# A third chunk lent to the seventh expert, the mask added out of PSUM, and probabilities divided on ScalarE before plain transposes

## The chip, the core and the metric

The kernel runs on one core of one Trainium2 chip. The metric is device time in microseconds (us) of one execution. Everything is float32; products of the front are made from two-part (high and low) float32r numbers to keep precision, those of the experts in plain float32.

## The reference, cut to what matters

One layer of an encoder over 256 tokens of width 1024: a combined projection, three attentions side by side, a gated merge, and a top-4-of-32 expert layer.

```python
h = rms_norm(x, attn_norm_g[l]); proj = h @ w_in[l]        # q, k, v of three branches, three gates
# A: 8 heads of 64 on a (4 x 64) token grid, window of 16 columns, bias by offset
# B: 12 heads of 64 in three groups (dilation 1, 4, 16), T5 bias, one softmax over the three groups
# C: 4 heads of 128 over 256 memory tokens
p = softmax(s + bias)            # per head; 256 x 256 scores; out = p @ v
merged = sum(gate_b * (branch_b @ w_branch_b)); x = x + merged @ w_out[l]
# experts: h = rms_norm(x); top 4 of 32 by router
gu = xb @ w_gu[e] + b_gu[e]      # 1024 -> 2048, 8 MB of weights per expert
g = min(gu[:, :1024], 7); u = clip(gu[:, 1024:], -7, 7)
a = (u + 1) * (g * sigmoid(1.702 * g)); y = a @ w_dn[e] + b_dn[e]     # 4 MB per expert
x = x + y_weighted; return rms_norm(x, final_norm_g)
```

## The kernel before, in words

All engine programs are written out by hand, each engine in its own order, with semaphores between them. Two parts follow each other.

**The front.** A list `FRONT` of 42 weight chunks of 1 MB (memory, input projection, branch and output weights) goes through a ring of 6 slots. SyncE (SP) issues all loads in one queue, chunk i when chunk i-6 is used (`chunk_used`). For each chunk ScalarE makes the high part (`high_part`, L1060, two halves), GpSimd the low part by subtraction (L568, two halves), and TensorE makes three products high-high, low-high, high-low; the last needs the low part (`parts_of_chunk`, L690). `high_part(i+2)` stands in ScalarE's iteration i, since the parts have two buffers. "Wide" pairs of chunks fill whole rows of 512.

The attention is a pipeline laid between chunks: `STEP_AFTER` says after which chunk i step s comes. There are 12 units of two heads: two C, four A, six B (groups 1 and 2 of B, `own_parity`, have half the keys: 128 columns in place of 256). Step s does on TensorE, in this order, `head_scores(s)` (L598), `turn_probs(s-3)` (L620) and `attend(s-4)` (L641). On VectorE (from L1345) it adds the relative image and, for A, the column mask `na_mask` (L1371), takes the row maximum (L1373) and its negative (`neg_max`, L1381), copies half of the turned probabilities (L1388), and at the steps of `SCALE_AT` inverts the sums of an output (L1397) and multiplies the identity by them (L1401). On ScalarE `exps(u)` (L1080) stands at the end of the step's iteration once all units of an output have their scores, and copies of the other half (L1159) and of the output (L1169) beside it. `turn_probs` turns the unnormalised exponentials by a matmul against a diagonal matrix of inverse sums, so that division and transpose are one operation; it waits for `scale_ready`.

**The experts.** 32 experts, 12 chunks of 1 MB each (8 gate/up, 4 down), in one order made by `transfers()` (L158), stream through a ring of 20 slots; chunk c is loaded when chunk c-20 and those beside it in one transfer are used. TensorE does gate/up of expert n and then down of n-1. Between the front and the experts the tokens are normalised (GpSimd and ScalarE, L573, L1188), routed and gathered. SP's order there: `FIRST_LAP` (chunks 2, 12, 14, 18, 16), a wait for the normalised tokens (`normed`, `tile_normed`, `sums_open`), the lent chunks, chunk 20, the stream.

Two chunks of the sixth expert, `LENT`, don't go through the ring. They are loaded early to memory that is idle by then (the tokens `x`, the bias staging, small tables), and `weights_landed` (L923) waits for them by semaphores of their own. After them, `x` takes the down bias and the final gain, which `DOWN_BIAS_AT` adds in four of the experts.

## Time and profile before

| | us |
|---|---|
| median of 3 runs | 1232.18 (1231.66 to 1232.54) |
| profiled execution, its own time | 1229.89 |
| span of that execution in the trace | 1228.1 |
| TensorE busy | 1174.6 (96%), 6225 instructions |
| VectorE busy | 267.5 (22%) |
| ScalarE busy | 253.0 (21%) |
| GpSimd busy | 207.2 (17%) |
| HBM read | 453.13 MB, 370 GB/s over the span |

Busy shares are averages over two stages with different limits; GpSimd's work, for one, lies wholly in the first quarter. An instruction's duration in a row contains its latency, so that for instructions in a row the distance between starts is less than the mean duration. The granted clock of TensorE is 0.987 of full speed in the mean. In the page's second part the span is cut into 40 slices of 30.7 us; the digits there are tenths.

### The profile page before, as it was taken

Reading aid. Unit: us, or ns where it says so; the run is one execution under the profiler, and the core shown is the slowest. Engines: PE = TensorE matmul, PEld = TensorE weight load, DVE = VectorE, ACT = ScalarE, POOL = GpSimd, SP = SyncE. Lnnn points to the kernel's source line nnn. Section 1 sums busy time; section 2 is a strip of 40 time slices with the busy share of each in tenths; the row PEclk is TensorE's granted clock in tenths of the full one; section 3 lists DMA queues with packets and bytes.
Section 4 is the critical chain, followed back from the end, with each engine's and each line's share of the span. In section 5 each row is a group of like instructions: output and inputs, shape, how many; then the busy total and the mean of one; then the engine's idle time right before and its main releaser. Section 6 shows DMA issues by size and latency. Waiting matters only on the chain.

```text
span 1228.1 us, 14301 instructions
## 1 busy us (share of the span) xinstructions
PE 1174.6 (96%) x6225; PEld 605.9 (49%) x6225; DVE 267.5 (22%) x543; ACT 253.0 (21%) x531; POOL 207.2 (17%) x89
## 2 busy tenths in 40 slices
PE   8999999999999999999999999999998998999996
PEld 8989887899433433333333333333333333333332
DVE  3148252232411112111111121111111111111112
ACT  6446455344301011100101010000100000000101
POOL 5865766686100000000000000000000000000000
PEclk9999999999999999999999999999999999999999
DMA  9753544599999999999999999999999999999995
GB/s 316 241 168 122 167 155 137 185 357 389 347 428 430 425 430 415 430 430 429 432 432 431 428 430 431 430 429 430 433 429 431 427 432 428 430 429 427 430 427 231
DMA packets 61703, 455.14 MB, mean 371 GB/s; under 512 B 5081, under 2 KB 33657, under 8 KB 43464
## 3 DMA queue, kind: packets, MB, share of 16 engines
q1 hardware_dynamic: 61640, 454.22, 90.0%
q8 instruction: 50, 0.82, 0.3%
q14 instruction: 13, 0.11, 0.0%
HBM read 453.13 MB, written 1.07 MB: 370 GB/s over the span
## 4 chain that ended last, share of the span: by engine, by line
PE 63%; DMA 33%; DVE 1%; POOL 1%; ACT 1%; issue 0%; DVEq 0%; SPq 0%; ACTq 0%; POOLq 0%
PE ps L579 62%; DMA arena<-in_expert_w_gate_up 29%; DMA arena<-in_expert_w_down 3%; POOL w_parts L568 1%; PE ps L895 1%; PE ps L889 0%; DVE arena L1371 0%; DMA arena<-in_mem 0%; DVE x_normed L1542 0%; PE ps L702 0%; PE ps L586 0%; ACT arena L1087 0%; PE ps L679 0%; DVE arena L1401 0%; DVE arena L1267 0%
## 5 line engine op out<-in xcount | busy, mean ns | idle before, releaser
L579 PE MATMUL ps<-arena,gathered_T 128*64 128x512 f32 x2034 | 471.2, 611 | 36.3 <-DMA arena<-in_expert_w_gate_up 36.3
L579 PE MATMUL ps<-arena 128*64 128x512 f32 (+8 forms) x1650 | 335.7, 534 | 4.1 <-DVE arena L1401 1.6
L579 PEld LDWEIGHTS ps<-arena,gathered_T 128*64 128x64 f32 x2034 | 144.9, 140 | 302.0 <-issue 273.3
L579 PEld LDWEIGHTS ps<-arena 128*64 128x64 f32 (+3 forms) x1650 | 132.2, 153 | 198.9 <-issue 191.6
L568 POOL TENSOR_TENSOR w_parts<-arena,w_parts 128x1024 fp32r<-128x1024 f32 x42 | 102.9, 2474 | 46.8 <-ACT w_parts L1067 37.7
L568 POOL TENSOR_TENSOR w_parts_odd<-arena,w_parts_odd 128x1024 fp32r<-128x1024 f32 x38 | 90.8, 2409 | 45.7 <-ACT w_parts_odd L1067 45.7
L1486 DVE TENSOR_SCALAR arena<-arena 128x128 f32<-128x128 f32 x64 | 19.3, 344 | 315.3 <-PE ps L889 315.3
L1209 ACT COPY arena<-ps 128x256 f32<-128x256 f32 x32 | 11.9, 372 | 358.8 <-PE ps L889 358.8
L1492 DVE TENSOR_SCALAR arena<-ps 128x512 f32<-128x512 f32 x32 | 22.1, 692 | 273.1 <-PE ps L579 273.1
L579 PEld LDWEIGHTS ps<-arena,x_normed 128*128 128x128 f32 x512 | 59.5, 192 | 24.8 <-issue 24.3
L1200 ACT ACTIVATE gathered_T<-ps,g_cols 128x128 f32<-128x128 f32 x128 | 36.5, 368 | 170.1 <-PE ps L579 170.1
L579 PE MATMUL ps<-arena,x_normed 128*128 128x128 f32 x512 | 65.4, 281 | 0.2 <-DVE arena L1443 0.2
L579 PE MATMUL ps<-w_parts_odd,h_T_parts 128*128 128x256 f32 (+1 forms) x360 | 59.1, 322 | 0.0
L1501 DVE COPY arena<-ps 128x512 f32<-128x512 f32 x32 | 22.1, 691 | 155.1 <-PE ps L895 155.1
L579 PEld LDWEIGHTS ps<-w_parts_odd,h_T_parts 128*128 128x128 f32 x360 | 51.5, 188 | 7.1 <-issue 1.8
L1217 ACT COPY arena<-ps 128x512 f32<-128x512 f32 x31 | 18.2, 586 | 172.3 <-PE ps L579 172.3
L1067 ACT CAST w_parts<-arena 128x1024 fp32r<-128x1024 f32 x40 | 39.9, 1047 | 49.2 <-PE ps L579 49.0
L1067 ACT CAST w_parts_odd<-arena 128x1024 fp32r<-128x1024 f32 x38 | 37.9, 1047 | 40.8 <-PE ps L579 40.3
L1213 ACT ACTIVATE arena<-arena 128x512 f32<-128x512 f32 x32 | 20.3, 633 | 109.6 <-DVE arena L1492 109.6
L579 PE MATMUL ps<-w_parts,h_T_parts 128*128 128x512 f32 (+1 forms) x216 | 41.1, 347 | 0.0
L579 PEld LDWEIGHTS ps<-w_parts,h_T_parts 128*128 128x128 f32 x216 | 33.7, 188 | 6.2 <-issue 0.6
L579 PE MATMUL ps<-h_T_parts,w_parts 128*128 128x256 f32 x288 | 35.5, 282 | 0.0
(181 smaller groups left out, 727.1 us busy)
## 6 DMA issues: line engine op xcount, KB each, us to landing
arena<-in_expert_w_gate_up SPq DMA_DIRECT2D x53, 4096.0 KB, 39.4
arena<-in_expert_w_down SPq DMA_DIRECT2D x62, 2048.0 KB, 38.8
arena<-in_expert_w_gate_up SPq DMA_DIRECT2D x21, 2048.0 KB, 12.4
arena<-in_w_in SPq DMA_DIRECT2D x29, 1024.0 KB, 5.4
arena<-in_w_out SPq DMA_DIRECT2D x4, 1024.0 KB, 11.3
arena<-in_expert_w_down SPq DMA_DIRECT2D x4, 1024.0 KB, 41.0
arena<-in_w_mem_kv SPq DMA_DIRECT2D x3, 1024.0 KB, 12.3
arena<-in_w_branch_a SPq DMA_DIRECT2D x2, 1024.0 KB, 5.1
```

Source lines behind the costliest of these rows:

```text
L568: last = nc.gpsimd.tensor_tensor(parts_at(i)[:, 1, half], ring[:, i % FRONT_RING, half], parts_at(i)[:, 0, half].bitcast(F32), ALU.subtract)
L579: return nc.tensor.matmul(out, lhsT, rhs, start=start, stop=stop, **kw)
L895: last = nc.tensor.transpose(ps[:, 2, f * P:(f + 1) * P], sig.rearrange("p (q f) -> p f q", f=4)[:, f, :], ident[:])
L1067: nc.scalar.copy(parts_at(i)[:, 0, half], ring[:, i % FRONT_RING, half]).then_inc(high_ready, 1)
L1200: last = nc.scalar.mul(xt[:, c, 0:width], ps[:, bank, k * P:k * P + width], g_cols[:, 3 * KC + c:3 * KC + c + 1])
L1209: nc.scalar.copy(WT[:, wt_slot, :], ps[:, 3, 0:S]).then_inc(WT_ready, 1)
L1213: nc.scalar.activation(sig, gate_c, ACT.Sigmoid, scale=ALPHA).then_inc(sig_ready, 1)
L1217: nc.scalar.copy(y_sb, ps[:, bank, :]).then_inc(y_ready, 1)
L1486: last = vec.tensor_scalar(PW[:, tt, :].rearrange("p (a s) -> p a s", a=2), bcast(slots, 1, 2), key_tile[:, tt, e], w_sel[:, tt, e], ALU.i ...
L1492: vec.tensor_scalar(gate_c, ps[:, 0, :], LIMIT, None, ALU.min).then_inc(gate_ready, 1)
L1501: vec.tensor_copy(aT, ps[:, 2, :].rearrange("p (f s) -> p f s", f=4)).then_inc(aT_ready, 1)
```

## The change

Three edits, with what they need.

- `LENT` has three chunks (5, 6 and 7 of gate/up) of the seventh expert in place of two of the sixth; `transfers()` splits that expert's second transfer so that each of them stands alone. The third goes to `behind_work`, the last 2048 columns of a working area 240 columns longer, which the merged tokens' parts occupy until the last chunk of the front is used; SP issues it behind `FIRST_LAP`, ahead of the wait for the normalised tokens. The down bias is added from expert 10 on.
- A units: VectorE adds the image in place in PSUM, then the mask with PSUM as source and SBUF as destination; `scores_drained` is raised after the mask.
- `turn_probs` makes plain transposes of probabilities that are already divided. ScalarE's `divide(u)` multiplies the exponentials of a unit by the inverse sums in place, at the head of the iteration of step u+3, ahead of `high_part(i+2)`. VectorE makes only the inverse (`inverse_ready`); `scaled_ident` is gone.
- Memory: row statistics move to the working area, `y_sb` becomes the same memory as `gate_c`, for which `move_down` waits for two more semaphores.

```diff
--- before.py
+++ after.py
@@ -52,7 +52,7 @@
 SCORE_SLOT = 8
 SECOND_SPLIT_SLOT = 10
 FRONT_SLOT = 12
-FRONT_WORK = 22784
+FRONT_WORK = 23024
 LATE_PARTS = (39, 41)
 IMAGES = 3
 EXPERT_CHUNKS = 12
@@ -93,15 +93,15 @@
 T5_STORE_AFTER = 11
 STEP_SLOT = {s: i for i, s in STEP_AFTER.items()}
 
-DOWN_BIAS_AT = {9: (0, 0), 10: (0, 1), 11: (1, 0), 12: (1, 1)}
+DOWN_BIAS_AT = {10: (0, 0), 11: (0, 1), 12: (1, 0), 13: (1, 1)}
 IMAGE_AFTER = {u: 9 if u < 2 + IMAGES else STEP_SLOT[u - IMAGES] + FRONT_RING for u in range(2, NU)}
 
 EARLY_AFTER = {36: 0, 38: 4, 39: 6, 40: 8, 41: 10}
 FIRST_LAP = {2: 38, 12: 38, 14: 40, 18: 41, 16: NF}
 FIRST_LONG = 4
 
-LENT_TO = 5
-LENT = (EXPERT_CHUNKS * LENT_TO + 2, EXPERT_CHUNKS * LENT_TO + 3)
+LENT_TO = 6
+LENT = tuple(EXPERT_CHUNKS * LENT_TO + j for j in (1, 2, 3))
 
 QK_DONE, QKV_DONE = {"C": 6, "A": 10, "B": 18}, {"C": 6, "A": 12, "B": 21}
 
@@ -161,7 +161,7 @@
     end_down = [(KC, 2), (KC + 2, 1), (KC + 3, 1)]
     order = [(0, *t) for t in short]
     for n in range(1, EXPERTS):
-        lent = [(0, 4), (4, 2), (6, 1), (7, 1)]
+        lent = [(0, 4), (4, 1), (5, 1), (6, 1), (7, 1)]
         order += [(n, *t) for t in (lent if n == LENT_TO else long if FIRST_LONG <= n < EXPERTS - 1 else short)]
         order += [(n - 1, *t) for t in (down if n < EXPERTS - 1 else end_down)]
     order += [(EXPERTS - 1, *t) for t in end_down]
@@ -214,10 +214,6 @@
         pick_raw = sb("pick_raw", [P, 2, EXPERTS + 1])
         sumsq = sb("sumsq", [P, 4, T])
         rstd = sb("rstd", [P, 4, T])
-        row_max = sb("row_max", [P, NU, 4])
-        neg_max = sb("neg_max", [P, 8, 4])
-        exp_sum = sb("exp_sum", [P, NU, 4])
-        inv_sum = sb("inv_sum", [P, 8, 4])
         ovf = sb("ovf", [P, MAX_OVERFLOW + 1], I32)
         b_tmp = sb("b_tmp", [P, 2, 4])
 
@@ -247,11 +243,13 @@
         pT = area(FRONT0, 2, 2, 2, S)
         image = area(FRONT0 + 2048, IMAGES, 2, IMG)
         na_mask = area(FRONT0 + 2048 + IMAGES * 2 * IMG, 4, GRID_W // 2)
+        stats_at = FRONT0 + 4096
+        row_max, exp_sum = area(stats_at, NU, 4), area(stats_at + 64, NU, 4)
+        neg_max, inv_sum = area(stats_at + 128, 8, 4), area(stats_at + 192, 8, 4)
         v = area(FRONT0 + 4352, T, 1280)
         mv = area(FRONT0 + 6912, T, MEM_HEADS * MEM_HD)
         qkT = area(FRONT0 + 8192, 24, S)
         mkT = area(FRONT0 + 14336, MEM_HEADS, MEM)
-        scaled_ident = area(FRONT0 + 15360, 2, 4, P)
         gates = area(FRONT0 + 16384, T, D)
         onehot = area(FRONT0 + 4352, REL)[0:T5_BUCKETS + 3, :]
         t5_in = area(FRONT0 + 4864, DIL_HEADS)[0:T5_BUCKETS + 3, :]
@@ -299,7 +297,7 @@
         assert place[0] <= FRONT0 + 18688
         router_parts = area(place[0], S)
         sig = moe(512)
-        y_sb, aT = moe(512), moe(4, P)
+        y_sb, aT = gate_c, moe(4, P)
         wT_sel = moe(S)[0:EXPERTS, :]
         pick = split_at("pick", place[0], 2, 2 * BLK)
         moe(2 * 2 * BLK)
@@ -312,6 +310,8 @@
         okeys = moe(T, EXPERTS)
         extra, ends = moe(EXPERTS), moe(EXPERTS)
         ovf_f = moe(MAX_OVERFLOW)
+        behind_work = area(FRONT0 + FRONT_WORK - CHUNK, CHUNK)
+        assert place[0] <= FRONT0 + FRONT_WORK - CHUNK
         final_g, far_iota, b_dn = x[:, 0, :], x[:, 1, :], x[0:EXPERTS, 1, :]
         final = xn[:]
 
@@ -346,7 +346,7 @@
         probs_exp = sem("probs_exp")
         front_evac, wide_done = sem("front_evac"), sem("wide_done")
         scores_ready, scores_drained = sem("scores_ready"), sem("scores_drained")
-        max_ready, exp_done, scale_ready = sem("max_ready"), sem("exp_done"), sem("scale_ready")
+        max_ready, exp_done, inverse_ready, divided = sem("max_ready"), sem("exp_done"), sem("inverse_ready"), sem("divided")
         probs_turned, pT_dve, pT_act = sem("probs_turned"), sem("pT_dve"), sem("pT_act")
         pv_done, out_high, out_low = sem("pv_done"), sem("out_high"), sem("out_low")
         merged_ready = sem("merged_ready")
@@ -380,7 +380,8 @@
 
         x_flat = x[:].rearrange("p t c -> p (t c)")
         bias_flat = bias_raw[:].rearrange("p b c -> p (b c)")
-        lent_pieces = {LENT[0]: [bias_flat[:, 0:512], bias_flat[:, 512:1024], until_ranked[:], until_routed],
+        lent_pieces = {LENT[2]: [behind_work[:, 512 * i:512 * (i + 1)] for i in range(4)],
+                       LENT[0]: [bias_flat[:, 0:512], bias_flat[:, 512:1024], until_ranked[:], until_routed],
                        LENT[1]: [x_flat[:, 512 * i:512 * (i + 1)] for i in range(4)]}
 
         def piece(c, i):
@@ -510,16 +511,18 @@
 
             sp.wait_ge(merged_ready, 4)
             sp.dma_start(iota, bass.AP(t["iota"].tensor, 0, [[0, P], [1, BLK]])).then_inc(iota_in, 16)
+            def lend(c, first, n, place):
+
+                e, j, _ = TRANSFERS[c]
+                src = w_gu[bass.ds(e, 1), :, j * CHUNK + 512 * first:j * CHUNK + 512 * (first + n)].rearrange("o p c -> (o p) c")
+                sp.dma_start(place, src).then_inc(lent_in[c], 16)
+
             for c, used in FIRST_LAP.items():
                 sp.wait_ge(chunk_used, used)
                 if used == NF:
                     load_bias()
                 load_weights(*TRANSFERS[c], ring_slot(c))
-            def lend(c, first, n, place):
-
-                e, j, _ = TRANSFERS[c]
-                src = w_gu[bass.ds(e, 1), :, j * CHUNK + 512 * first:j * CHUNK + 512 * (first + n)].rearrange("o p c -> (o p) c")
-                sp.dma_start(place, src).then_inc(lent_in[c], 16)
+            lend(LENT[2], 0, 4, behind_work)
 
             sp.wait_ge(normed, 3)
             sp.wait_ge(tile_normed, 1)
@@ -618,8 +621,7 @@
                 last.then_inc(scores_ready, 1)
 
             def turn_probs(u):
-                o = OUTPUT_OF[u]
-                pe.wait_ge(scale_ready, o + 1)
+                pe.wait_ge(divided, u + 1)
                 if u == 0:
                     pe.wait_ge(t5_copied, 1)
                 else:
@@ -628,14 +630,12 @@
                 for hh in range(2):
                     if own_parity(u):
                         for tt in range(T):
-                            last = mm(ps[:, 6 + hh, tt * P:(tt + 1) * P], scores[:, u % 4, hh, tt, 0:P],
-                                      scaled_ident[:, o % 2, 2 * hh + tt, :], True, True)
+                            last = nc.tensor.transpose(ps[:, 6 + hh, tt * P:(tt + 1) * P], scores[:, u % 4, hh, tt, 0:P], ident[:])
                         continue
                     for kt in range(T):
                         for tt in range(T):
-                            last = mm(ps[:, 6 + hh, kt * S + tt * P:kt * S + (tt + 1) * P],
-                                      scores[:, u % 4, hh, tt, kt * P:(kt + 1) * P], scaled_ident[:, o % 2, 2 * hh + tt, :],
-                                      True, True)
+                            last = nc.tensor.transpose(ps[:, 6 + hh, kt * S + tt * P:kt * S + (tt + 1) * P],
+                                                       scores[:, u % 4, hh, tt, kt * P:(kt + 1) * P], ident[:])
                 last.then_inc(probs_turned, 1)
 
             def attend(u):
@@ -923,7 +923,7 @@
             def weights_landed(c):
 
                 if c in LENT:
-                    pe.wait_ge(lent_in[c], {LENT[0]: 48, LENT[1]: 16}[c])
+                    pe.wait_ge(lent_in[c], {LENT[0]: 48, LENT[1]: 16, LENT[2]: 16}[c])
                 else:
                     pe.wait_ge(landed[ring_slot(c)], 16 * fills_through(c))
 
@@ -1088,6 +1088,15 @@
                                                     accum_out=exp_sum[:, u, 2 * hh + tt:2 * hh + tt + 1])
                 last.then_inc(exp_done, 1)
 
+            def divide(u):
+                o = OUTPUT_OF[u]
+                act.wait_ge(inverse_ready, o + 1)
+                for hh in range(2):
+                    for tt in range(T):
+                        p = scores[:, u % 4, hh, tt, 0:P if own_parity(u) else S]
+                        last = nc.scalar.mul(p, p, inv_sum[:, o, 2 * hh + tt:2 * hh + tt + 1])
+                last.then_inc(divided, 1)
+
             def move_wide(i, tt):
 
                 kind, n = FRONT[i - 1]
@@ -1109,6 +1118,8 @@
                     act.wait_ge(wide_done, WIDE_LAST.index(i) + 1)
                     move_wide(i, 0)
                 merging = ONLY_B < i < OUT0
+                if i in STEP_AFTER and 0 <= STEP_AFTER[i] - TURN_LAG < NU:
+                    divide(STEP_AFTER[i] - TURN_LAG)
                 if i + 2 < NF and not merging:
                     high_part(i + 2)
                 if i - 1 in STEP_AFTER and STEP_AFTER[i - 1] in LAST_OF_B:
@@ -1212,8 +1223,10 @@
                 act.wait_ge(gate_ready, n + 1)
                 nc.scalar.activation(sig, gate_c, ACT.Sigmoid, scale=ALPHA).then_inc(sig_ready, 1)
 
-            def move_down(chunks, bank):
+            def move_down(chunks, bank, n):
                 act.wait_ge(chunk_used, chunks + NF)
+                act.wait_ge(prod_ready, n + 1)
+                act.wait_ge(sig_ready, n + 1)
                 nc.scalar.copy(y_sb, ps[:, bank, :]).then_inc(y_ready, 1)
 
             for n in range(EXPERTS):
@@ -1223,7 +1236,7 @@
                     move_gathered(n % 2, XT[:, (n // 2 + 1) % 2], 2 * BLK, n + 2)
                 sigmoid(n)
                 if n:
-                    move_down(down_chunk(n - 1) + 4, 3)
+                    move_down(down_chunk(n - 1) + 4, 3, n)
             move_weights(EXPERTS - 1, (EXPERTS - 1) % 2)
             n_over = act.value_load(ovf[0:1, MAX_OVERFLOW:MAX_OVERFLOW + 1], min_val=0, max_val=MAX_OVERFLOW)
             with act.If(0 < n_over):
@@ -1233,7 +1246,7 @@
                             move_gathered(half, XT[:, 0], BLK, b * 2 + (EXPERTS + half))
                         move_weights(b + EXPERTS, 1)
                         sigmoid(b + EXPERTS)
-                        move_down(b * EXPERT_CHUNKS + (ALL_CHUNKS + EXPERT_CHUNKS), 3)
+                        move_down(b * EXPERT_CHUNKS + (ALL_CHUNKS + EXPERT_CHUNKS), 3, b + EXPERTS)
 
             nc.scalar.activation(b_tmp[:, 0, 0:1], eps[:], ACT.Sqrt)
             for tt in range(T):
@@ -1352,7 +1365,7 @@
                             dve.wait_ge(image_in[b], 16 * ((s - 2) // IMAGES + 1))
                         for tt in range(T):
                             src = ps[:, 2:4, tt * S:(tt + 1) * S]
-                            dst = scores[:, s % 4, :, tt, :]
+                            dst = src if kind_u == "A" else scores[:, s % 4, :, tt, :]
                             if kind_u == "C":
                                 last = vec.tensor_copy(dst, src)
                             elif own_parity(s):
@@ -1362,13 +1375,16 @@
                                 rel = image[:, b, :, 1 - tt:1 - tt + S].rearrange("p h (j e) -> p h e j", e=2)
                                 by_parity = "p h (e j) -> p h e j"
                                 last = vec.tensor_tensor(dst.rearrange(by_parity, e=2), src.rearrange(by_parity, e=2), rel, ALU.add)
+                        if kind_u == "A":
+                            link(last)
+                            dve.wait_ge(consts_in, 96)
+                            by_column = "p (t e r c) -> p (t e) r c"
+                            for hh in range(2):
+                                biased = ps[:, 2 + hh, :].rearrange(by_column, t=T, e=2, c=GRID_W // 2)
+                                masked = scores[:, s % 4, hh].rearrange("p t k -> p (t k)").rearrange(by_column, t=T, e=2, c=GRID_W // 2)
+                                last = vec.tensor_tensor(masked, biased, bcast(na_mask[:], 2, 4), ALU.add)
                         last.then_inc(scores_drained, 1)
                         dve.wait_ge(scores_drained, s + 1)
-                        if kind_u == "A":
-                            dve.wait_ge(consts_in, 96)
-                            for hh in range(2):
-                                masked = scores[:, s % 4, hh].rearrange("p t (e r c) -> p (t e) r c", e=2, c=GRID_W // 2)
-                                link(vec.tensor_tensor(masked, masked, bcast(na_mask[:], 2, 4), ALU.add))
                         width = P if own_parity(s) else S
                         link(vec.tensor_reduce(row_max[:, s, :], scores[:, s % 4].rearrange("p h t k -> p (h t) k")[:, :, 0:width],
                                                AX_X, ALU.max))
@@ -1394,12 +1410,7 @@
                         if UNITS[w][0] == "B":
                             total = b_tmp[:, 1, :]
                             link(vec.tensor_reduce(total, exp_sum[:, w - 2:w + 1, :].rearrange("p u c -> p c u"), AX_X, ALU.add))
-                        link(vec.reciprocal(inv_sum[:, o, :], total))
-                        if o >= 2:
-                            dve.wait_ge(probs_turned, last_unit_of(o - 2) + 1)
-                        for c in range(4):
-                            last = vec.tensor_scalar(scaled_ident[:, o % 2, c, :], ident[:], inv_sum[:, o, c:c + 1], None, ALU.mult)
-                        last.then_inc(scale_ready, 1)
+                        vec.reciprocal(inv_sum[:, o, :], total).then_inc(inverse_ready, 1)
                     u = s - PV_LAG
                     if 0 <= u < NU and u == last_unit_of(OUTPUT_OF[u]):
                         dve.wait_ge(out_high, OUTPUT_OF[u] + 1)
```

## Rows read from the trace of the kernel before

**Rows 1.** The page: the chain's shares, and GB/s in 40 slices of the span.
```profile
PE 63%; DMA 33%; DVE 1%; POOL 1%; ACT 1%; issue 0%; DVEq 0%; SPq 0%; ACTq 0%; POOLq 0%
...
GB/s 316 241 168 122 167 155 137 185 357 389 347 428 430 425 430 415 430 430 429 432 432 431 428 430 431 430 429 430 433 429 431 427 432 428 430 429 427 430 427 231
```

**Rows 2.** The chain in order of time: start, length, what.
```profile
649.30 37.10 DMA arena<-in_expert_w_gate_up
```

**Rows 3.** Windows: length, then each engine's busy time, PEclk, DMA share, GB/s.
```profile
305.00:310.00 5.00, 4.66 (x30) 2.50 (x30) 2.63 (x12) 4.36 (x9) 2.39 (x1) 1.00 0.83 217
310.00:315.00 5.00, 4.82 (x27) 3.08 (x26) 4.12 (x23) 2.48 (x4) 1.46 (x1) 1.00 0.92 368
315.00:320.00 5.00, 5.00 (x36) 3.46 (x37) 4.52 (x15) 2.28 (x8) 0.00 (x0) 1.00 0.89 344
320.00:325.00 5.00, 5.00 (x25) 1.61 (x22) 1.96 (x11) 0.00 (x0) 0.00 (x0) 1.00 0.55 192
```

**Rows 4.** Timeline of the SP queue between front and experts: start, length, issue.
```profile
307.27 0.58 SPq L440 DMA_DIRECT2D arena<-in_expert_w_down  x1
313.76 0.33 SPq L522 DMA_DIRECT2D x_tokens<-in_expert_w_gate_up  x1
...
321.51 0.33 SPq L440 DMA_DIRECT2D arena<-in_expert_w_gate_up  x1
```

**Rows 5.** DMA issues, KB, us to landing; from 391 to 398, then 417 to 425.
```profile
arena<-in_expert_w_down SPq DMA_DIRECT2D x2, 2048.0 KB, 17.5
...
arena<-in_expert_w_down SPq DMA_DIRECT2D x2, 2048.0 KB, 15.7
```

**Rows 6.** Products of probabilities and merge transposes: groups to 330 us, timeline, chain.
```profile
L579 PE MATMUL ps<-arena 128*128 128x128 f32 x160 | 20.7, 281 | 1.7 <-DVE arena L1401 1.6
...
L702 PE MATMUL ps<-ident,x_normed 128*128 128x128 f32 x16 | 2.4, 272 | 0.0
...
91.28 2.05 PE L579 MATMUL ps<-arena 128*128 128x128 f32 x16 [1.63 <-DVE arena L1401]
...
267.65 0.44 PE ps L702 x4
```

**Rows 7.** VectorE groups to 330 us: busy, mean ns, then idle before them.
```profile
L1371 DVE TENSOR_TENSOR arena<-arena 128x512 f32<-128x512 f32 x8 | 15.3, 1913 | 0.3
L1373 DVE TENSOR_REDUCE row_max<-arena 128x4 f32<-128x1024 f32 x8 | 9.8, 1220 | 0.3
...
L1364 DVE TENSOR_TENSOR arena<-ps,arena 128x512 f32<-128x512 f32 x12 | 7.7, 682 | 36.0 <-PE ps L579 36.0
...
L1381 DVE TENSOR_SCALAR neg_max<-row_max 128x4 f32<-128x4 f32 x6 | 5.7, 942 | 0.2
```

**Rows 8.** ScalarE groups to 330 us, scalings by a column vector.
```profile
L1056 ACT ACTIVATE h_T_parts<-ps,g_cols 128x256 fp32r<-128x256 f32 x8 | 3.0, 489 | 0.0
...
L1200 ACT ACTIVATE gathered_T<-ps,g_cols 128x128 f32<-128x128 f32 x8 | 2.3, 368 | 4.3 <-PE ps L579 4.3
```

**Rows 9.** Timeline of all engines around step 3.
```profile
82.84 1.29 DVE L1364 TENSOR_TENSOR arena<-ps,arena 128x512 f32<-128x512 f32 x2 [13.24 <-PE ps L579]
83.01 5.22 POOL L568 TENSOR_TENSOR w_parts<-arena,w_parts 128x1024 fp32r<-128x1024 f32 x2 [0.74 <-ACT w_parts L1067]
...
88.52 1.13 PE L579 MATMUL ps<-arena 64*128 64x256 f32 x8
...
90.27 0.51 ACT L1087 ACTIVATE arena<-arena,neg_max 128x256 f32<-128x256 f32 x1 [6.45 <-DVE neg_max L1381]
...
92.25 0.56 ACT L1098 COPY arena<-ps 128x512 f32<-128x512 f32 x1
```

**Rows 10.** Timeline of TensorE at step 5, of ScalarE and TensorE at step 9.
```profile
109.36 4.84 PE L579 MATMUL ps<-arena 64*128 64x256 f32 x32
...
175.00 1.28 ACT L1102 ACT_TABLE_LOAD   x1
...
176.87 4.31 PE L579 MATMUL ps<-arena 64*128 64x256 f32 x32
```

## The prediction

> **What bounds the kernel now.** I read the page's chain first: 63% of it is TensorE and 33% DMA, and the GB/s line says where each rules: below 200 in slices 3 to 8, then about 430 from the twelfth slice to the last but one [rows 1]. In order of time the chain first stands on an expert weight transfer at 649.30 [rows 2]; before that it is nearly all TensorE. So there are two regimes: the front (attention, to about 305 us) goes at TensorE's pace, the experts in the end at the DMA's.
>
> What matters is from when the DMA is saturated. In windows of 5 us it moves 217, 368, 344 and 192 GB/s between 305 and 325 [rows 3]. The SP queue says why: it issues a chunk at 307.27, the next thing at 313.76 (it waits for the normalised tokens), and chunk 20, which opens the endless stream, at 321.51, when TensorE has used the first two expert chunks [rows 4]. After that the DMA is always behind its slots. The end is therefore (issue of chunk 20) + (bytes after it) / rate + tail, and two things move it: the front's length, one for one, and bytes taken out of the stream.
>
> **The third lent chunk.** The ring holds 20 chunks; a lent chunk is loaded to other memory ahead of the stream and later left out of it. Leaving one out is worth 1.049 MB / 430 GB/s = 2.44 us. Does its load find idle DMA? It is issued behind chunk 16, at 307.9. From 310 to 325 the DMA gives away 5 x (62 + 86 + 238) / 430 = 4.5 us against 430 GB/s [rows 3], so 2.44 fits, and ahead of chunk 20 too: the 1.8 MB issued between 313.76 and 316 need 4.3 us. Does the omission find a backlog? The down transfers of one expert land 17.5 us after their issue, those of the next, with two chunks left out between, 15.7 [rows 5]: the backlog grows by 15.7 + 4.9 - 17.5 = 3.1 per expert. Now three are left out one expert later and none before: 17.5 + 3.1 + 3.1 - 7.3 = 16.4, so the queue doesn't run dry there. Worth -2.4 us; bounds 0 (if it pushes chunk 20 back by its whole length) and -2.5. The expert after which the down bias and the final gain are fetched only shifts their 0.64 MB. That the down result shares memory with `gate_c` adds waits on products that end while the 32 down matmul instructions before that copy still run: 0.
>
> **Plain transposes.** `turn_probs` makes 8 products of 128x128 for eight of the units and 4 for the four others: 80, which are 160 instructions in the group of this shape [rows 6]; 16 of them took 2.05 us at 91.28, 0.128 each. A transpose is one instruction: 4 take 0.44 us in the merge, 0.11 each [rows 6]. What goes is thus every second instruction, 80 x 0.11 = -8.8 us of TensorE time, all in the part of the front in which TensorE is the chain. Bounds: -10.2 (by 0.128), and 0 if a transpose of such an operand holds the array for two slots after all.
> The Trainium skill (TensorE: Matmul & The Clock Gate, Part 4: PE-mode transpose) speaks against it: about 275 ns for a transpose in a kernel, and transposes don't count as busy time for the clock. Laid end to end at that price the 80 would cost 22 us, more than the products. The trace agrees with the figure as the duration of one transpose and not as the price of each in a row, and the window 305 to 310, with transposes in it, has a granted clock of 1.00 [rows 3, 6].
>
> **Mask out of PSUM.** In each of the four A units VectorE adds the image (out of PSUM, 0.68 a time), then the mask, SBUF to SBUF: 1.91 us on average, 2.8 times as long for the same size [rows 7]. It stands beside GpSimd's subtractions, and the one with a PSUM source doesn't suffer. Out of PSUM I take 0.69, bounds 0.65 and 1.91; 8 x 1.2 = -9.8 us of VectorE time. The image addition now writes PSUM, which no row shows: I take 0.68, bounds 0.6 and 1.9. The scalings of the identity go from VectorE, a reciprocal stays. `neg_max` stays too, and 0.94 on average for 128x4 [rows 7] says that it also waits for GpSimd, so of what the mask gives a part is given back: `neg_max` ends when GpSimd's pair ends. That is off TensorE's path except where the walk below says.
>
> **Divides on ScalarE.** The nearest rows are scalings of 128x256, 8 in 3.0 us, and of 128x128, 8 in 2.3 [rows 8]: 1.6 us for a full unit (three at 0.375, the last to its end 0.49), 1.25 for a small one, 8 x 1.6 + 4 x 1.25 = 17.8 us more ScalarE work. Bounds for a full one 1.2 and 2.1. `divide` is queued behind the exps of the step before (which wait for `neg_max`) and ahead of `high_part(i+2)`. TensorE waits for it in `turn_probs`; behind that stand `attend` and the next chunk. Step by step:
> - Step 3. The scores of unit 2 are there at 82.84. Image 1.3, mask 1.4, maximum 1.2: 86.8; `neg_max` then waits for GpSimd, whose pair begins at 83.01 and takes 4.8 undisturbed (5.22 now): 87.9. Exps and the gap to the evacuation 2.0 (90.27 to 92.25), evacuation 0.6, divide 1.6: 92.2. TensorE has the scores of unit 3 out at 88.52 + 1.13 = 89.65 and waited until 91.28 before [rows 6, 7, 9]. Loses 0.9 more.
> - Step 4. Exps after the first GpSimd subtraction of chunk 13, 96.0 to 98.1, divide to 99.7; TensorE is free at 100.1: 0.
> - Step 5. GpSimd's pair for chunk 14 runs to 105.5, so `neg_max` 105.6, exps to 107.7, copy of C 0.5, divide to 109.8; TensorE is free at 109.6 (109.36 + 1.05 now, less 0.8 of lead) [rows 10]. Loses 0.2.
> - Step 9. A table load of 1.28 (at 175.00) and a sigmoid of 0.6 stand ahead of the divide [rows 10]; with the front 4.2 ahead 170.8 + 1.9 + 1.6 = 174.3, and TensorE is there at 173.7. Loses 0.6, and 0.2 of that it loses now. Step 12 has the same pattern with its exps done: 0.2.
> - In the other eight steps the divide is over before TensorE has finished the chunk: 0.
> Sum 0.9 + 0.2 + 0.4 + 0.2 = 1.7, and the front -8.8 + 1.7 = -7.1 (with 2.1 for a divide -5.1; with no wait left -10.4). `high_part` comes up to 1.6 late, but GpSimd has until 2 us into chunk i+2, with chunk i+1 (5.8) and a step's 2 to 4 us before that, and needs 1.0 + 4.8: some 4 to 5 us of slack. Were that cover gone, each divide would be paid in full (rival 2). SP's wait for `scores_drained` ahead of an image load ends 1.4 later in A units, with the next front load due some 4 us after: 0.
>
> Sum: -7.1 - 2.4 = -9.5 us. The profiled execution took 1229.89 around its span of 1228.1; the median of the runs is 1232.18, 0.2% more. The sum is a difference, and I set it against the median: 1222.7.
>
> **Rivals.**
> 1. *The divide becomes the new wait.* In the dense steps of the A and B units it ends 1.0 late in six instead of in one. For it: steps 3 and 5 are on the edge. Against: from 142 us on the exps lie away from the next step. Front -8.8 + 6 = -2.8, in all -5.2: 1227.0.
> 2. *Slower: high parts come late.* If GpSimd's low part of chunk i+2 is what TensorE waits for, each step pays its whole divide: -8.8 + 17.8 - 2.4 = +6.6, 1238.8. It decides from a delay of 4 to 5 us, where I count 1.6.
> 3. *The lent chunk brings nothing*, its load pushing chunk 20 back: -7.1, 1225.1.
> 4. *Transposes don't run closer than the products.* With two slots each the front changes by 0 to +1.7 (longer turns leave the divides more time), with -2.4 in all -1.5: 1230.7, no change. Laid end to end at their own duration, 0.272 [rows 6]: 80 x 0.272 - 17.6 = +4.2, with 1.7 and -2.4 +3.5, 1235.7, slower. Against both: 4 in 0.44.
>
> **Chances.** Forecast 0.67 (its own range 1220 to 1225.5), rival 1 0.12, rival 3 0.08, rival 2 0.04, rival 4 0.06 at no change and 0.03 slower. What this measurement can tell from no change is about 0.2%, 2.5 us: faster 0.87, same 0.06, slower 0.07. The range reaches from -13 (no wait left and both at their better bounds) to the far edge of rival 1: 1219 to 1229.
>
> **What would show it.** The products of the probabilities: 80 instructions in place of 160. Masks at 0.69 in the VectorE group, with PSUM as source. TensorE waits for ScalarE's divide 2.5 us at its first turn, under 1 at two or three others, and not for GpSimd at the steps. Chunk 20 issued 7 us earlier, near 314.4, with 1 MB more moved in the 15 us before it. The forecast is wrong if chunk 20 is issued less than 4 us earlier, or if it is and the end isn't, which would say that the stream's rate or its backlog is not what I take.

## The result, and the profile after

| | before | after |
|---|---|---|
| median of 4 runs, same chip (us) | 1231.92 (1230.72 to 1232.54) | 1218.21 (1216.15 to 1219.22) |
| profiled execution, its own time | 1229.89 | 1218.18 |
| span | 1228.1 | 1216.4 |
| chunk 20 issued | 321.51 | 314.81 |
| last transfer on the chain landed | 1200.75 | 1187.83 |
| very last weights landed | 1215.51 | 1202.47 |

The ratio is 0.9889, 95% interval 0.9875 to 0.9904: 13.7 us faster, where 9.5 were forecast. The direction was right; the time lies 0.8 us below the low end of the range. So something gave 4 us that the sum did not have.

Of the page of after, the chain's shares, to set beside [rows 1]; then the chain in order of time (start, length, what), its first expert transfer and its last transfer:

```profile
PE 66%; DMA 30%; ACT 1%; DVE 1%; issue 1%; POOL 0%; SPq 0%; DVEq 0%; ACTq 0%; POOLq 0%
```

```profile
695.52 38.56 DMA arena<-in_expert_w_gate_up
...
1149.36 38.47 DMA arena<-in_expert_w_down
```

The two regimes are still there, and the end still follows the transfers. "The chain" is the page's chain of work that ended last; behind its last transfer five more land, up to 15 us later, while TensorE still works. The chain comes onto the DMA 46 us later than in [rows 2].

Windows of after, columns as in [rows 3]:

```profile
305.00:310.00 5.00, 4.84 (x37) 3.98 (x37) 4.46 (x18) 1.35 (x4) 0.00 (x0) 1.00 0.97 408
310.00:315.00 5.00, 5.00 (x29) 2.34 (x29) 4.55 (x20) 1.72 (x7) 0.00 (x0) 1.00 0.94 383
315.00:320.00 5.00, 5.00 (x24) 1.65 (x22) 0.36 (x2) 0.00 (x0) 0.00 (x0) 1.00 0.88 324
320.00:325.00 5.00, 5.00 (x32) 2.78 (x30) 0.00 (x0) 0.53 (x3) 0.00 (x0) 1.00 1.01 426
```

The SP queue of after, to set beside [rows 4]; the second line is the third lent chunk, the last chunk 20:

```profile
300.57 0.58 SPq L441 DMA_DIRECT2D arena<-in_expert_w_down  x1
301.20 0.43 SPq L518 DMA_DIRECT2D arena<-in_expert_w_gate_up  x1
307.06 0.33 SPq L518 DMA_DIRECT2D x_tokens<-in_expert_w_gate_up  x1
...
314.81 0.33 SPq L441 DMA_DIRECT2D arena<-in_expert_w_gate_up  x1
```

Chunk 20 goes out 6.7 us earlier in after, so these windows don't stand at the same place of the work as those of [rows 3]. Set side by side by the work, in the 15 us that end with the issue of chunk 20 the DMA moves 370 GB/s at a share of 0.98, where it moved 295 at 0.84: 1.1 MB more, which is the third lent chunk. The hole is filled.

The groups of after up to 330 us (columns as in [rows 6 to 8]): the transposes, the two additions of the A units, `neg_max`, the divides:

```profile
L1097 ACT ACTIVATE arena<-arena 128x256 f32<-128x256 f32 x32 | 13.6, 500 | 0.0
L1397 DVE TENSOR_SCALAR arena<-arena 128x4 f32<-128x4 f32 x6 | 10.1, 1690 | 0.2
L637 PE MATMUL ps<-ident,arena 128*128 128x128 f32 x64 | 8.7, 280 | 3.0 <-ACT arena L1097 2.9
...
L1377 DVE TENSOR_TENSOR ps<-ps,arena 128x512 f32<-128x512 f32 x8 | 5.2, 698 | 19.6 <-PE ps L582 19.6
L1385 DVE TENSOR_TENSOR arena<-ps,arena 128x512 f32<-128x512 f32 x8 | 5.2, 686 | 0.1
L1097 ACT ACTIVATE arena<-arena 128x128 f32<-128x128 f32 x16 | 5.1, 400 | 0.0
...
L633 PE MATMUL ps<-ident,arena 128*128 128x128 f32 x16 | 2.5, 279 | 0.0
```

There are 64 + 16 = 80 transposes in 8.7 + 2.5 = 11.2 us, where [rows 6] had 160 instructions in 20.7. The mask takes 0.69 us instead of 1.91 [rows 7], the addition that writes PSUM 0.70, and `neg_max` 1.69 instead of 0.94: it still ends when a subtraction of GpSimd ends.

### The profile page after: what moved, and what is told of

Same layout as the page of the kernel before. It is cut to its first block, busy times and chain, and to the rows that moved or that the text cites. A ratio compares the mean times of both kernels' runs of the same rounds, so it can differ in the third digit from the quotient of the medians.

```text
span 1216.4 us, 14183 instructions
## 1 busy us (share of the span) xinstructions
PE 1163.0 (96%) x6145; PEld 594.5 (49%) x6145; DVE 249.1 (20%) x511; ACT 269.5 (22%) x579; POOL 206.1 (17%) x89
## 3 DMA queue, kind: packets, MB, share of 16 engines
HBM read 453.13 MB, written 1.07 MB: 373 GB/s over the span
## 4 chain that ended last, share of the span: by engine, by line
PE 66%; DMA 30%; ACT 1%; DVE 1%; issue 1%; POOL 0%; SPq 0%; DVEq 0%; ACTq 0%; POOLq 0%
PE ps L582 63%; DMA arena<-in_expert_w_gate_up 26%; DMA arena<-in_expert_w_down 3%; PE ps L895 1%; PE ps L637 1%; PE ps L889 1%; DMA arena<-in_w_mem_kv 1%; POOL w_parts L571 0%; ACT arena L1097 0%; ACT arena L1087 0%; ACT L1111 0%; ACT w_parts L1067 0%; DVE x_normed L1553 0%; PE ps L633 0%; PE ps L702 0%
## 5 line engine op out<-in xcount | busy, mean ns | idle before, releaser
L582 PE MATMUL ps<-arena 128*64 128x512 f32 (+6 forms) x1490 | 316.4, 562 | 3.6 <-issue 2.3
L582 PEld LDWEIGHTS ps<-arena 128*64 128x64 f32 (+3 forms) x1490 | 113.3, 149 | 196.3 <-issue 193.7
## 6 DMA issues: line engine op xcount, KB each, us to landing
arena<-in_w_mem_kv SPq DMA_DIRECT2D x3, 1024.0 KB, 11.2
```

The costliest lines, as they stand in the source:

```text
L582: return nc.tensor.matmul(out, lhsT, rhs, start=start, stop=stop, **kw)
```

## Where the 13.7 us came from

The two profiled executions differ by 11.7 us, and three stretches of their traces hold it: chunk 20 is issued 6.7 earlier (314.81, 321.51); from that issue to the landing of the last transfer on the chain it takes 873.02 instead of 879.24, 6.2 less; and the tail behind is 1.2 longer. Of the first, TensorE came to the front 2.0 late: at the start it waited 2.5 us instead of 0.7 for VectorE's parts of the memory tokens (`mem_T_parts`). VectorE came to them late, because its two casts of the first weight chunk, beside GpSimd's first subtraction, took 3.67 us instead of 1.28. The profiled executions below show the one or the other (the casts end late in after, e1, e4, e6 and e11, early in the others), so it is no part of the change; I call it the long and the short start. From the scores of unit 2 (81.66 and 83.64) to chunk 20 there are 239.85 us before and 231.17 after: -8.7, where I had -7.1 (0.8 of it turns out to be the address, see e5 to e7). Of the second, the lent chunk should give 2.4. The other 3.8 us were in no step of mine: the same bytes went in less time.

What differs for them is where they land. The change moves the four row statistics, 640 bytes in each partition, from ahead of the large area, which starts at `base`, into it. So the rings of weight chunks, and everything else in that area, start 640 bytes lower: 38912 instead of 39552. The first is a multiple of 512, the second is 128 past a multiple of 256; the line that sets `base` rounds to 64 only. The list of the change in front of the prediction names the move, but not that the rings shift by it.

## The experiments

Each kernel was timed in five rounds beside the one before; those of a set share its runs (medians 1231.66, 1231.66 and 1230.85 in the first, second and third set). e1 to e4 are the first set, e5 to e8 the second, the others the third. e10 is told beside e4, with which it shares a question.

**e1_memory**: only the moves of memory, with the waits that the shared `y_sb` needs.

```diff
-FRONT_WORK = 22784
+FRONT_WORK = 23024
-        row_max = sb("row_max", [P, NU, 4])   # and neg_max, exp_sum, inv_sum
+        stats_at = FRONT0 + 4096
+        row_max, exp_sum = area(stats_at, NU, 4), area(stats_at + 64, NU, 4)
+        neg_max, inv_sum = area(stats_at + 128, 8, 4), area(stats_at + 192, 8, 4)
-        y_sb, aT = moe(512), moe(4, P)
+        y_sb, aT = gate_c, moe(4, P)
```

> Only the memory moves of the change: row statistics in the working area (which is 240 columns longer, so that everything behind them shifts by 640 bytes), the down result in the memory of gate_c with its two more waits. Nothing in the front, two lent chunks as before. Theory A (the time missed is front work and stall that I priced too low, and nothing lies in the stream): 0, within 1 us of before. Theory B (the new places in memory make the expert stream itself faster, since from chunk 20 to the last landing the changed kernel gained 6.2 us where one lent chunk explains 2.4): 2 to 4 us faster, with the same time from the first step to chunk 20.

Measured: 1226.43 (1225.26 to 1227.55), ratio 0.9957 (0.9944 to 0.9971): -5.2 us from a part that I had put at nothing. Chunk 20 goes out at 322.63, not earlier than before (the long start is in it); from there to the landing of the last transfer on the chain it takes 875.69, 3.6 us less than before.

**e2_lent**: e1 and the third lent chunk with its new expert.

```diff
-LENT_TO = 5
-LENT = (EXPERT_CHUNKS * LENT_TO + 2, EXPERT_CHUNKS * LENT_TO + 3)
+LENT_TO = 6
+LENT = tuple(EXPERT_CHUNKS * LENT_TO + j for j in (1, 2, 3))
+            lend(LENT[2], 0, 4, behind_work)   # ahead of chunk 20
```

> Memory moves and the third lent chunk for the seventh expert, nothing in the front. Theory A: -2.4 us against before. Theory B: -2.4 and what the memory moves alone give, -4.5 to -6.5. If omitting chunks is worth more than their bytes (theory C), this is more than 2.4 below the run with the memory moves alone, which is then at 0.

Measured: 1222.98 (1222.68 to 1223.61), ratio 0.9933 (0.9920 to 0.9947), 3.4 us below e1. The other pair with and without it, after and e3, differs by 1.5. The two stand on either side of the 2.4 forecast. The traces are closer: from the scores of unit 2 to chunk 20 there are 239.15 us in e2 and 239.18 in e1, so the load doesn't push chunk 20 back, and the stream behind it is 2.0 shorter in the mean of all kernels with three lent chunks (table below).

**e3_front**: the changed kernel with two lent chunks, as before.

```diff
-LENT_TO = 6
-LENT = tuple(EXPERT_CHUNKS * LENT_TO + j for j in (1, 2, 3))
+LENT_TO = 5
+LENT = (EXPERT_CHUNKS * LENT_TO + 2, EXPERT_CHUNKS * LENT_TO + 3)
-            lend(LENT[2], 0, 4, behind_work)
```

> The changed kernel with the lent chunks of before: two, of the sixth expert, but all of the front's edits and the memory moves. Theory A: the front gives about -8.7 (what the trace shows between the scores of unit 2 and the issue of chunk 20), and the changed kernel's -13.7 would then be -11.2 here with the lent chunk's 2.4 taken off, if the rest lies in the front's other places. Theory B: -8.7 and 2 to 4 from the memory moves, -11 to -12.5, chunk 20 issued 8.7 earlier, the rest gained after it. The two are told apart by the run with the memory moves alone.

Measured: 1219.68 (1218.30 to 1220.73), ratio 0.9903 (0.9888 to 0.9918), 6.75 us below e1. Chunk 20 goes out at 313.93, 7.6 before that of before, both with the short start.

**e4_turns**: e3, but the mask still from SBUF to SBUF: transposes and divides alone.

```diff
-                            dst = src if kind_u == "A" else scores[:, s % 4, :, tt, :]
+                            dst = scores[:, s % 4, :, tt, :]
...
-                                last = vec.tensor_tensor(masked, biased, bcast(na_mask[:], 2, 4), ALU.add)
+                                link(vec.tensor_tensor(masked, masked, bcast(na_mask[:], 2, 4), ALU.add))
```

> Memory moves, divides and plain transposes, but the mask still added SBUF to SBUF, and two lent chunks. Theory A: the mask edit is worth only what it takes off the stalls: neg_max then comes 0.9 to 3 us later in steps 2 to 5, the divide behind it too, so TensorE waits some 2 us at each of steps 3, 4 and 5 in place of 2.4, 0 and 0.1. 3 to 5 us slower than the run with all of the front's edits. A rival holds that the mask edit is worth nothing, since neg_max is pinned to GpSimd's end either way: the same within 1 us.

Measured: 1227.58 (1225.45 to 1228.88), ratio 0.9964 (0.9950 to 0.9977): 7.9 us above e3 and 1.2 above e1, whose interval overlaps its own, so against e1 no difference is shown. The divides at the head of the steps eat what the transposes give, unless the mask becomes shorter too. The timeline of e4 at its first turn, VectorE and TensorE:

```profile
85.12 4.60 DVE L1379 TENSOR_TENSOR arena<-arena 128x512 f32<-128x512 f32 x2
89.75 1.22 DVE L1381 TENSOR_REDUCE arena<-arena 128x4 f32<-128x1024 f32 x1
...
95.42 1.97 PE L632 MATMUL ps<-ident,arena 128*128 128x128 f32 x8 [4.80 <-ACT arena L1092]
97.04 7.65 PE L577 MATMUL ps<-h_T_parts,w_parts 128*128 128x256 f32 x48
```

and the windows of that stretch (PEclk is the third number from the end):

```profile
92.00:96.00 4.00, 0.58 (x3) 0.58 (x4) 3.20 (x5) 4.00 (x12) 0.00 (x0) 0.77 0.75 261
96.00:100.00 4.00, 4.00 (x21) 4.00 (x20) 0.77 (x2) 4.00 (x12) 3.56 (x2) 0.50 0.01 4
100.00:104.00 4.00, 4.00 (x32) 4.00 (x32) 0.00 (x0) 1.79 (x6) 1.16 (x1) 0.87 0.00 0
```

Two masks take 4.60 us beside GpSimd, and TensorE waits 4.8 us for the divide. Then the granted clock is 0.50, the 1.2 GHz level, for the window behind the wait, and the 48 instructions of the next chunk take 7.65 instead of 5.90 (after, below). So one late divide costs 4.8 and then 2.6 more: 1.75 in the chunk, 0.9 in the eight transposes (1.97, and 1.09 in after). A second wait, of 2.18, stands at step 5.

**e10_mask**: e1 and the mask out of PSUM, with the old products.

```diff
-                            dst = scores[:, s % 4, :, tt, :]
+                            dst = src if kind_u == "A" else scores[:, s % 4, :, tt, :]
...
-                                link(vec.tensor_tensor(masked, masked, bcast(na_mask[:], 2, 4), ALU.add))
+                                last = vec.tensor_tensor(masked, biased, bcast(na_mask[:], 2, 4), ALU.add)
```

> Memory moves (rings at a multiple of 512 bytes) and the mask out of PSUM; the turns are products with the scaled identity as before, two lent chunks. Theory A (the mask edit is worth what it takes off a wait behind it): the first turn's wait of 1.6 goes or shrinks, since neg_max is there 1 to 3 us earlier, and no other: 1 to 2 us faster than the memory moves alone, 1224.5 to 1225.5. The difference between the runs e3 and e4, 7.9 us, was then the divide's: the mask is worth so much only with the divide behind it. Rival: the mask is worth 4 or more by itself.

Measured: 1223.72 (1222.91 to 1227.23), ratio 0.9944 (0.9931 to 0.9957), against 0.9957 for e1: worth 1.6 us by the ratios and at most 2.7 by the medians, and their intervals overlap. TensorE's wait of 1.63 at the first turn [rows 6] is gone, and chunk 20 goes out at 318.78, 2.7 before that of before (0.8 of that comes with the new addresses, see below). With e4: the turns alone give nothing (1.2 slower, within the noise), the mask alone gives 1.6 to 2.7, both give 6.75. The two parts belong together, since it is the mask that gives the divide its time.

**e5_aligned, e6_shift128, e7_shift256**: the disputed 640 bytes by themselves. e5 is before with only the four statistics moved into the large area; e6 and e7 put 128 and 256 unused bytes ahead of the area again.

```diff
-        row_max = sb("row_max", [P, NU, 4])   # and the three others; e5, e6, e7
+        stats_at = FRONT0 + 4096              # as in e1
+        sb("pad", [P, 32])                    # e6 only; [P, 64] in e7
```

> The kernel before with only the four row statistics moved into a hole of the working area. That takes 640 bytes away in front of the rings, so that they begin at a multiple of 512 bytes (38912) in place of 128 beyond one (39552). Theory B1 (the start address of the rings in SBUF sets the time of each packet: the trace of before has 32 KB packets of 1219 on average and a median of 1215 ns, every kernel with the moves 1216 and 1213): 3.5 to 5 us faster, packets of 1213. Rival B2 (the memory shared by the down result, or its waits, is what helped): 0.

> The same with 128 unused bytes ahead of the rings (39040, 128 beyond a multiple of 512, as in the kernel before). Theory B1: back to the time of before within 1 us, packets slow again. Rival B2 and any theory in which moving the statistics helps by itself: as the aligned kernel.

> The same with 256 unused bytes (39168, 256 beyond a multiple of 512). If packets want 256-byte lines the time is that of the aligned kernel; if they want 512, that of before. I take 512, with 0.35.

| kernel | rings start | mod 256 | us (lowest to highest) | ratio (95%) |
|---|---|---|---|---|
| before | 39552 | 128 | 1231.66 (1229.72 to 1233.64) | |
| e5 | 38912 | 0 | 1225.38 (1224.20 to 1228.04) | 0.9953 (0.9939 to 0.9967) |
| e6 | 39040 | 128 | 1230.92 (1229.63 to 1233.59) | 0.9997 (0.9988 to 1.0006) |
| e7 | 39168 | 0 | 1224.86 (1224.38 to 1225.29) | 0.9944 (0.9931 to 0.9957) |

This settles that the address is the cause. Same instructions, same number of them; 128 bytes take all of the gain away and 256 give it back. That 256 is enough went against my expectation for e7, which had taken 512. The statistics' move itself is worth nothing: e6 has it and is not faster.

Windows of one stretch in the stream, 330 to 1190 us, of before, e6, e5 and e7 in that order:

```profile
330.00:1190.00 860.00, 822.63 (x3891) 316.12 (x3891) 135.42 (x301) 83.89 (x212) 0.00 (x0) 0.98 1.00 429
```

```profile
330.00:1190.00 860.00, 822.89 (x3894) 316.69 (x3892) 135.51 (x301) 84.02 (x212) 0.00 (x0) 0.98 1.00 429
```

```profile
330.00:1190.00 860.00, 827.93 (x3897) 317.12 (x3895) 136.09 (x303) 84.24 (x213) 0.00 (x0) 0.98 1.00 431
```

```profile
330.00:1190.00 860.00, 827.98 (x3902) 316.76 (x3904) 136.12 (x303) 84.22 (x213) 0.00 (x0) 0.98 1.00 431
```

The DMA share is 1.00 in all four: the engines are as good as never idle, they only move 429 GB/s or 431. Half a per cent over 879 us is 4 us. The records of the single packets, from the traces, say it more finely:

| packets | count | before | e6 | e5 | e7 | e1 |
|---|---|---|---|---|---|---|
| 32 KB, mean ns | 6784 | 1219.4 | 1219.8 | 1216.9 | 1216.7 | 1215.9 |
| 16 KB, mean ns | 10674 | 621.5 | 621.7 | 618.8 | 618.9 | 618.1 |

About 3 ns more for each packet, small or large: a price per packet, not per byte. 17458 packets x 3 / 16 engines = 3.3 us. The stretch from the issue of chunk 20 to the landing of the very last weights is the same measure in all kernels:

| rings, mod 256 | lent chunks | us from the issue of chunk 20 to the very last landing | mean |
|---|---|---|---|
| 128 | 2 | before 894.0, e6 893.9, e9 894.4 | 894.1 |
| 0 | 2 | e1 890.3, e3 889.4, e4 889.5, e5 890.8, e7 890.0, e10 889.8 | 890.0 |
| 0 | 3 | after 887.7, e2 888.0, e8 888.8, e11 888.3, e12 887.4 | 888.0 |

The address is worth 4.1 us there, a little more than the packets explain, and the third lent chunk 2.0. The Trainium skill (DMA: Bandwidth & Descriptors, How a descriptor splits into AXI transactions) gives the rule that I should have weighed: a transaction must start at a 256-byte boundary, so a descriptor that starts off one gets a first transaction with unused bytes, which still cost beats of 32 bytes. The page tells it of the side that is read, and here it is the side written that moved. 128 unused bytes are four beats; at the clock of the page's bandwidth sum (850 MHz) an estimate from the page is 4.7 ns a packet. The runs agree with a price per packet and put it at 3, and they agree with the boundary as far as they go: 0 and 256 past a multiple of 512 are fast, 128 past is slow, and no other remainder was tried.

By the medians the address is worth 5.2 to 6.8 us, more than these 4.1. Another 0.8 lies in the front: from the scores of unit 2 to chunk 20 it is 239.85 us in before and 239.84 in e6, but 238.98 in e5, 239.01 in e7 and 239.18 in e1. Why is not shown. Profiled executions with the same short start differ by 4.4 (e5: 1225.51, before: 1229.89) and 5.0 (e7: 1224.86), those with the long start by 4.1 (e1: 1227.55, e6: 1231.67). That of before lies 1.8 below its own median, so that its other executions may have the long start more often than those of e5 and e7; that is argued, not shown, and the rest stays open.

**e9_front128**: e3, shifted back onto the old remainder, so the front's terms alone.

```diff
-FRONT_WORK = 23024
+FRONT_WORK = 22784
+        sb("pad", [P, 32])
```

> All of the front's edits and the places of the down result, with two lent chunks of the sixth expert, and 128 unused bytes ahead of the rings so that they begin 128 beyond a multiple of 512, as before: the terms of the prediction's front alone. By the traces so far the front's part is -6.5 to -8 at the issue of chunk 20, +1.3 in the tail, so -5 to -7 against before: 1225 to 1226.5. If the address and the front's edits work on one another (the address slows the front's own loads too, say) it is nearer to before, 1228.

Measured: 1226.42 (1223.74 to 1227.10), ratio 0.9958 (0.9945 to 0.9971): -4.4 us from before, and 6.7 above e3: the shift costs at least as much on the changed front. Chunk 20 goes out at 313.95, 7.6 before that of before, and from the scores of unit 2 to it there are 232.04 us instead of 239.85: with the address held, the front's edits give 7.8 there. The profiled execution, the fastest of the five, is 6.15 below that of before (1223.74, 1229.89): part of the front's gain does not arrive at the end.

**The tail.** That part goes in the last products. TensorE and VectorE at the end, first of before, then of after, then of e3:

```profile
1218.07 0.69 DVE L1513 COPY arena<-ps 128x512 f32<-128x512 f32 x1 [8.69 <-PE ps L579]
1219.08 1.99 PE L579 MATMUL ps<-arena 64*128 64x512 f32 x8 [1.05 <-DVE arena L1513]
```

```profile
1205.14 0.69 DVE L1524 COPY arena<-ps 128x512 f32<-128x512 f32 x1 [8.69 <-PE ps L582]
1207.36 1.99 PE L582 MATMUL ps<-arena 64*128 64x512 f32 x8 [2.27 <-issue]
```

```profile
1206.01 0.69 DVE L1519 COPY arena<-ps 128x512 f32<-128x512 f32 x1 [8.69 <-PE ps L577]
1208.36 3.67 PE L577 MATMUL ps<-arena 64*128 64x512 f32 x8 [2.39 <-issue]
```

Before, the products start 0.3 us behind the end of the copy; in after 1.5, and the profile puts the wait down to "issue". In e3 it is 1.66, and the products themselves take 3.67 instead of 1.99, at a granted clock of a half. From the landing of the last transfer on the chain to the end it takes 27.3 us before, 28.5 in after and 29.6 in e3: the tail costs 1.2 to 2.3 us that I had at nothing. e4 looks like e3 (1.59, then 3.68), and e9 lies between (1.36, then 2.64). All kernels with the old products (before, e1, e2, e5, e6, e7, e10) have the 0.3, all with the transposes 0.95 to 1.66. With the transposes TensorE's program is 80 instructions shorter, so what is issued at the end lies elsewhere in it.

**e8_early**: after, with less at the head of the critical steps. The inverses of the outputs 0 and 1 are taken at step 1, and their units are divided at the head of chunk 10, away from the first turn.

```diff
-SCALE_AT = {2: 0, 3: 1, 4: 2, 5: 3, 6: 4, 7: 5, 8: 6, 11: 7}
+SCALE_AT = {1: (0, 1), 4: (2,), 5: (3,), 6: (4,), 7: (5,), 8: (6,), 11: (7,)}
+DIVIDE_AT = {10: (0, 1), **{i: (s - TURN_LAG,) for i, s in STEP_AFTER.items() if 2 <= s - TURN_LAG < NU}}
-                if i in STEP_AFTER and 0 <= STEP_AFTER[i] - TURN_LAG < NU:
-                    divide(STEP_AFTER[i] - TURN_LAG)
+                for u in DIVIDE_AT.get(i, ()):
+                    divide(u)
```

> The changed kernel with the inverses of the first two outputs made at step 1 and units 0 and 1 divided at the head of chunk 10, where ScalarE has nothing to do, in place of steps 3 and 4. Theory A (the divide behind the exps of the step before is the one wait of the front that is left to take): TensorE doesn't wait at its first turn, 2.4 us less in the front, and no fall of the granted clock behind it (0.57 for 4 us in one trace of the front alone): chunk 20 is issued 2.4 to 4 us earlier and the kernel is 2.4 to 3.5 us faster than the changed one, near 1215. Rival: the exps of unit 3 and the divide of unit 2 come later because ScalarE or GpSimd is full there, and the wait moves to step 5: 0 to 1 us.

Measured: 1213.76 (1212.70 to 1215.11), ratio 0.9854 (0.9839 to 0.9869), 4.4 us below after: it beats both kernels. In its trace the first turn waits for nothing, and chunk 20 goes out at 310.15, 4.7 before that of after. Of that 2.1 are after's long start; from the scores of unit 2 to chunk 20 it is 228.63 instead of 231.17, so the wait gave 2.5, as theory A has it. Where the rest of the 4.4 comes from is open. In e3 a fall of the granted clock followed the same wait (last section), and some of after's other executions may have it; that is argued, not shown. The divides of units 0 and 1, and TensorE's only wait for a divide in the front (engine, line waited for: us in total, times, longest):

```profile
78.24 3.30 ACT L1098 ACTIVATE arena<-arena 128x256 f32<-128x256 f32 x8
```

```profile
PE ps L638 <- ACT arena L1098: 0.5, 1, 0.5
```

**e11_warm20, e12_warm14**: e8 with another number of warm-up products at the start, which puts all that follows at another place in TensorE's program.

```diff
-WARM = 18
+WARM = 20     # e12: WARM = 14
```

> The kernel with early divides and two more of TensorE's first throw-away products, which moves all its later instructions by 8 places. In the four kernels with plain transposes TensorE begins the last 4 products 1.1 to 1.6 us after the copy they wait for, in the others 0.3 after. If that hangs on where the instructions lie, the gap changes with the shift, to 0.3 or to another value between; if it is the transposes' doing, it stays at 1.1. Time within 1.5 us of the kernel with early divides.

> The same with four fewer of those products, all later TensorE instructions 16 places earlier. As for the run before: the gap ahead of the last products changes if it hangs on the place. The first transposes come at the same time, since they wait for the normalised memory tokens.

Measured: 1213.62 (1211.98 to 1215.49), ratio 0.9851 (0.9838 to 0.9863), and 1212.92 (1212.57 to 1213.85), ratio 0.9852 (0.9839 to 0.9864): no difference from e8. The gap before the last products is 1.14 in e8, 0.95 in e11 and 1.53 in e12. It moves with the place of the instructions but does not go back to 0.3. That it depends on the place is what this suggests; that the place is all of it is not shown, and what in the issue takes the time stays open.

## Why the prediction was wrong

**The step that failed** is in "What bounds the kernel now": the end is "(issue of chunk 20) + (bytes after it) / rate + tail, and two things move it", the front's length and the bytes. The rate was taken as fixed, and the moves of memory as worth nothing: of the shared `gate_c` I asked only which waits it adds and put it at 0, and the move of the row statistics stands in no term of the sum at all. With the four statistics the start of the rings went from 128 past a multiple of 256 to a multiple of 256, which is worth 5.2 to 6.8 us (e1, e5, e7; e6 takes it away). The sentence "The forecast is wrong if chunk 20 is issued less than 4 us earlier, or if it is and the end isn't, which would say that the stream's rate or its backlog is not what I take" named the right place, though as a reason to doubt a gain, not to find more of it. By the medians the 13.7 us split as 5.2 (e1), 6.75 (e3 less e1) and 1.5 (after less e3), with the intervals of e1, e3 and after each 3 to 4 us wide. Without the first, 8.3 are left where I had 9.5. Measured the other way, with the address held at its old remainder (e9), the front's edits give 4.4 (by the interval 3.6 to 6.8) instead of the 7.1 forecast, and with 1.5 to 3.4 for the lent chunk 5.9 to 7.8 are left. So the terms that I did name were forecast somewhat too large, and the loss in the tail hid a part of the address's gain: without it the time would lie further below the range.

The other steps:

- *What bounds the kernel*, but for the fixed rate: right. That the front's length counts one for one the long start shows by itself: e11 has it and e12 hasn't, chunk 20 goes out at 312.00 and 309.88, 2.1 apart, and their profiled executions took 1215.49 and 1212.92, 2.6 apart.
- *Third lent chunk, -2.4*: -3.4 and -1.5 by the medians and -2.0 by the stretches, right within what the runs can tell. Rival 3 is out. The load goes out at 301.20, in the hole; down transfers of the expert that leaves three out land 16.1 us after issue, where I had 16.4, so the backlog holds:

```profile
arena<-in_expert_w_down SPq DMA_DIRECT2D x2, 2048.0 KB, 17.8
...
arena<-in_expert_w_down SPq DMA_DIRECT2D x2, 2048.0 KB, 20.7
...
arena<-in_expert_w_down SPq DMA_DIRECT2D x2, 2048.0 KB, 16.1
```

- *Transposes, 0.11 for each that goes*: slightly low. The eight of one turn at 142 us with their products take 3.10 us instead of 4.06: 0.96, where 8 x 0.11 = 0.88. Rival 4 is out. The 275 ns of the Trainium skill (TensorE: Matmul & The Clock Gate, Part 4: PE-mode transpose), measured there in another kernel, are near the duration that the rows show here (280), not the price in a row (0.12).
- *Mask 0.69, addition into PSUM 0.68*: 0.686 and 0.698. That `neg_max` gives a part back is right, and stronger than I took it (1.69 on average).
- *Divides 1.6 and 1.25*: 1.7 for a full one, 1.3 for a small one. Step 3 in the timeline of after:

```profile
84.82 1.30 DVE L1377 TENSOR_TENSOR ps<-ps,arena 128x512 f32<-128x512 f32 x2 [13.13 <-PE ps L582]
84.99 4.79 POOL L571 TENSOR_TENSOR w_parts<-arena,w_parts 128x1024 fp32r<-128x1024 f32 x2 [0.63 <-ACT w_parts L1067]
86.15 1.29 DVE L1385 TENSOR_TENSOR arena<-ps,arena 128x512 f32<-128x512 f32 x2
88.73 1.07 DVE L1397 TENSOR_SCALAR arena<-arena 128x4 f32<-128x4 f32 x1
...
92.28 1.71 ACT L1097 ACTIVATE arena<-arena 128x256 f32<-128x256 f32 x4
94.04 1.09 PE L637 MATMUL ps<-ident,arena 128*128 128x128 f32 x8 [2.40 <-ACT arena L1097]
94.89 5.90 PE L582 MATMUL ps<-h_T_parts,w_parts 128*128 128x256 f32 x48
```

The wait is 2.40, where I had 2.5; `neg_max` ends at 89.80, with GpSimd's pair (89.78), as the walk has it. Step 9 waits 0.53 (forecast 0.6), step 5 under 0.1 and step 12 nothing (forecast 0.2 each). Over the whole front: 80 transposes at 0.12 are -9.6, the waits 2.9 in place of 1.6 are +1.3, so -8.3. The -8.7 measured between before and after contain the 0.8 of the address; with the address held (e9) it is -7.8, where the forecast had -7.1. Rivals 1 and 2 are out: there are two waits for a divide in the front, 2.9 us in all, and none for a high part.

- *The tail*: taken as unchanged, it costs 1.2 us in after and up to 2.3 (e3, e4).

The range was too narrow for one reason. Its low end held only the better bounds of terms that I had named; a term that I had not named, of 5 us, could not be in it, though that the rate stays the same rested on nothing that a row shows about other addresses.

## What to carry to other kernels

When an allocation moves, work out where the targets of the large transfers start, modulo 256 bytes, and round the base of the area to that: in a kernel whose DMA is the limit (share 1.00), 128 bytes were worth 5 to 7 us of 1232, as much as any edit of the code here. Before an operation is moved onto the head of a critical step, find the step in which it will be the last to arrive, and shorten what stands ahead of it (here the mask) or take it out of that step (e8): the transposes and divides without the shorter mask gave nothing. And an experiment that changes only one part must keep the addresses of the others, or it measures two.
